# Modulation sums, chunked projections and a moved broadcast in a two-block transformer kernel

## What is computed

```python
def hybrid_layer(x, c, ...):
    mod = silu(c) @ mod_w + mod_b                       # 1024 x 6144
    shift1, scale1, gate1, shift2, scale2, gate2 = split(mod, 6)
    h = rms_norm(x, g_pre_mix) * (1 + scale1) + shift1
    sc_b, sc_c, sc_x, q, k, v, z, xbc, dt, gl_a, gl_b, gl_c = split_columns(h @ w_in)
    y_a = short_conv_mixer(sc_b, sc_c, sc_x, sc_conv_w) @ w_sc_out
    y_b = stick_breaking_attention(q, k, v) @ w_sb_out
    y_c = mamba2_mixer(z, xbc, dt, ...) @ w_ssm_out     # conv, silu, decay scan, gated norm
    merged = sigmoid(gl_a) * y_a + sigmoid(gl_b) * y_b + sigmoid(gl_c) * y_c
    x = x + gate1 * rms_norm(merged @ w_o, g_post_mix)
    h2 = rms_norm(x, g_pre_ffn) * (1 + scale2) + shift2
    gt, up = split(h2 @ w_ffn_in, 2)
    return x + gate2 * rms_norm((silu(gt) * up) @ w_ffn_out, g_post_ffn)

def second_block(x, c, ...):    # own modulation; attention, pooling, then peer_ffn:
    ...                         # top-16 of 16384 experts per head and token, gathered rows
```

## Time and profile before

| what | us |
|---|---|
| median of 3 runs | 1389.44 (1386.64 to 1390.31) |
| profiled execution | 1389.17 |
| its span | 1387.4 |
| PE busy | 1157.2 (83%) |
| DVE busy | 906.1 (65%) |
| POOL busy | 432.2 (31%) |
| ACT busy | 249.1 (18%) |
| DMA | 412.99 MB, mean 298 GB/s |

### The profile page before, as it was taken

One profiled execution on the slowest core, in us unless ns is written; L12 is line 12 of the kernel. 1 busy time (PEld: TensorE's weight loads), 2 busy tenths in 40 slices (PEclk: granted clock), 3 DMA queues, 4 the chain that ended last, 5 costly groups with the idle time before them and its releaser, 6 DMA issues.

```text
span 1387.4 us, 13536 instructions
## 1 busy us (share of the span) xinstructions
PE 1157.2 (83%) x4534; PEld 759.1 (55%) x4534; DVE 906.1 (65%) x2145; ACT 249.1 (18%) x412; POOL 432.2 (31%) x351
## 2 busy tenths in 40 slices
PE   2999898985799997798798998787878778777786
PEld 2888787845699996774374563333323333333332
DVE  7334037257788886543268869687786968778556
ACT  1114121015233333432211100101010010101001
POOL 0000000012244443220032536444444445445440
PEclk9999999998899998798898999898989998999998
DMA  9447335363667776230259999999999999999994
GB/s 387 179 144 275 155 141 199 148 236 128 261 278 291 293 299 242 71 112 31 91 227 421 418 396 421 421 421 421 421 422 420 421 420 422 422 421 422 421 422 166
DMA packets 57220, 412.99 MB, mean 298 GB/s; under 512 B 6480, under 2 KB 6480, under 8 KB 7120
## 3 DMA queue, kind: packets, MB, share of 16 engines
q0 software_dynamic: 42912, 311.97, 54.7%
q1 hardware_dynamic: 14256, 100.37, 18.7%
HBM read 411.26 MB, written 1.05 MB: 297 GB/s over the span
## 4 chain that ended last, share of the span: by engine, by line
PE 49%; DMA 27%; DVE 16%; issue 4%; ACT 2%; POOL 1%; DVEq 0%; SPq 0%; POOLq 0%; ACTq 0%
PE ps L394 13%; PE ps L815 11%; DMA areaB<-in_experts,idx 6%; DMA gate_area<-in_experts,idx 5%; PE ps L407 5%; PE ps L409 5%; PE ps L408 5%; DMA hT<-in_experts,idx 4%; PE ps L474 4%; DVE mod_sum L1214 3%; DMA ring<-in_experts,idx 3%; DMA mod_ring<-in_experts,idx 3%; DMA mod_ring<-in_mod_w 2%; PE ps L622 2%; DMA spare<-in_experts,idx 2%
## 5 line engine op out<-in xcount | busy, mean ns | idle before, releaser
L394 PE MATMUL ps<-hT,ring 128*128 128x256 f32 x960 | 220.2, 391 | 1.5 <-ACT hT L863 1.5
L394 PEld LDWEIGHTS ps<-hT,ring 128*128 128x128 f32 x960 | 187.8, 197 | 30.6 <-issue 3.9
L815 PE MATMUL ps<-areaB,mod_sum 128*128 128x512 f32 x304 | 157.4, 667 | 39.0 <-DVE mod_sum L1655 39.0
L815 PE MATMUL ps<-gate_area,mod_sum 128*128 128x512 f32 x240 | 118.8, 644 | 32.1 <-DVE mod_sum L1655 32.1
L815 PEld LDWEIGHTS ps<-areaB,mod_sum 128*128 128x128 f32 x304 | 63.1, 213 | 127.0 <-issue 76.5
L1156 POOL DMA_INDIRECT areaB<-in_experts,idx x76 | 92.3, 1215 | 112.6 <-PE ps L815 105.8
L1058 ACT ACTIVATE act<-now 128x2 f32<-128x2 f32 (+1 forms) x130 | 26.4, 203 | 562.4 <-DVE now L1646 562.4
L407 PE MATMUL ps<-hT_h,w_lo 128*128 128x256 f32 x416 | 119.0, 286 | 4.1 <-DVE hT_l L1199 2.2
L815 PE MATMUL ps<-ring,mod_sum 128*128 128x512 f32 x188 | 95.2, 653 | 31.9 <-DVE mod_sum L1655 31.9
L1646 DVE CUSTOM_DVE_ANT_0 areaB<-areaB,xn 128x1024 f32<-128x1024 f32 x76 | 92.2, 1223 | 44.4 <-DMA areaB<-in_experts,idx 44.3
L1214 DVE SCALAR_TENSOR_TENSOR mod_sum<-mod_ring,cols,mod_sum 128x256 f32<-128x256 f32 x294 | 119.2, 481 | 0.0
(11 more groups left out here) (273 smaller groups left out, 1855.1 us busy)
## 6 DMA issues: line engine op xcount, KB each, us to landing
ring<-in_stream SPq DMA_DIRECT2D x84, 1024.0 KB, 5.7
mod_ring<-in_mod_w POOLq DMA_DIRECT2D x40, 1024.0 KB, 6.9
gate_area<-in_mod_w SPq DMA_DIRECT2D x3, 1024.0 KB, 12.8
areaB<-in_mod_w SPq DMA_DIRECT2D x3, 1024.0 KB, 19.2
mod_ring<-in_mod_w SPq DMA_DIRECT2D x2, 1024.0 KB, 6.0
small<-in_small SPq DMA_DIRECT2D x1, 1352.0 KB, 27.4
areaB<-in_experts,idx POOLq DMA_INDIRECT x76, 22.6
x_sb<-in_x SPq DMA_DIRECT2D x1, 1024.0 KB, 9.0
```

The lines of the kernel that those rows point to most:

```text
L394: last = mm(ps[:, bank, b * T:(b + 1) * T], w[:, at:at + P], rhs[:, k, :], start=(k == 0), stop=(k == KC - 1))
L815: last = mm(ps[:, B3 + 2 * t + b, :], spread_w[n // FEW % 2][:, n % FEW, :], row[ROW_OF[n]][:, D + 512 * b:D + 512 * b + 512], start=first ...
```

## The change

- `mod_sum` gets eight places, so a pair from 8 on waits only for `mod_used` m - 6 (at least 8). `MOD_FRONT` = 28: pairs 24 and 26 come before the FFN, and POOL loads units 8 to 29 in one loop ahead of all its `split_lo` steps.
- DVE's pairs stand at: 8 after `dt_lin`; 10 after `ya`; 12 and 14 after sb_lk; 16 and 18 after sba (L1368); 20 after the acs copy, ahead of the wait for `acs_mm`; 22 after the weighting; 24 ahead of the merges; 26 after them. PE sums 8 to 11 after gl 3, 12 to 15 after the acs_mm matmuls, 16 to 19 after gl 11, 20 to 27 after wo 3.
- Head: the first eight units are stored so that each pair holds the same 256 columns of shift1 and scale1. After each pair `early_columns` makes two chunks' columns (inside the next pair's products), ACT makes all eight hT chunks, and PE does xbc 0 to 2 in parts (`xbc_part`) as chunks arrive, in three banks. The dt matmuls come after sc 0. SP's order is now: pair 0, x, small constants, pairs 1 and 2, slots 0 and 1, pair 3, slot 2, late constants.
- The first gate-row broadcast is done in halves after wo 0 and wo 1.

```diff
+MOD_FRONT = 28
-        mod_sum = sb("mod_sum", 4 * T)
+        mod_sum = sb("mod_sum", 8 * T)
+        def early_bank(j):
+            return (BM, BX, BM, BM)[j]
         def sum_place(m):
-            return m % 4 if m < 24 else m % 2
+            if m < MOD_EARLY:
+                return m % 4
+            return m % 8 if m < MOD_FRONT else m % 2
...
+            load_pair(0)
+            sp.dma_start(x_sb, x).then_inc(x_in, 16)
+            sp.dma_start(sm[:, n_c:n_late], small[:, n_c:n_late]).then_inc(small_in, 16)
+            load_pair(1)
+            load_pair(2)
+            first_load(0)
+            first_load(1)
+            load_pair(3)
+            first_load(2)
...
             transposes(0)
-            mod_units(*range(2, 8))
+            mod_units(2, 3)
+            def xbc_part(j, *ks):
+                w = arrived("xbc", j)
+                for b in range(2):
+                    for k in ks:
+                        pe.wait_ge(hT_act, k + 1)
+                        at = (b * KC + k) * P
+                        last = mm(ps[:, (0, 1, BX)[j], b * T:(b + 1) * T], w[:, at:at + P], hT[:, k, :],
+                                  start=(k == 0 and b == 0), stop=(k == KC - 1), skip_group_check=True)
+                if KC - 1 in ks:
+                    last.then_inc(unit_done, 1)
+            xbc_part(0, 0, 1)
+            xbc_part(0, 2, 3)
+            mod_units(4, 5)
+            xbc_part(0, 4, 5)
+            xbc_part(1, 0, 1, 2, 3, 4, 5)
+            pe.wait_ge(mod_read, 2)
+            xbc_part(2, 0, 1)
+            mod_units(6, 7)
+            xbc_part(2, 2, 3, 4, 5)
             for j in range(3):
-                proj_T("xbc", j)
+                xbc_part(j, 6, 7)
+            proj_T("sc", 0)
+            pe.wait_ge(evac, 3)
...
                     last.then_inc(acs_mm, 1)
-                    mod_units(14, 15)
+                    mod_units(*range(12, 16))
...
-            pe.wait_ge(yms, 1)
-            broadcast_row(0)
+            mod_units(*range(16, 20))
...
                 wide("wo", j, mT)
-                if j in (0, 2):
-                    mod_units(20 + j, 21 + j)
+                if j < 2:
+                    broadcast_half(0, j)
+            mod_units(*range(20, MOD_FRONT))
...
                     elif m >= 4:
-                        dve.wait_ge(mod_used, m - 2 if m < 24 else m)
+                        dve.wait_ge(mod_used, m - 2 if m < MOD_EARLY else max(MOD_EARLY, m - 6))
...
+            def early_columns(j):
+                dve.wait_ge(small_in, 16)
+                dve.wait_ge(mod_used, 2 * j + 2)
...
+            for m in range(1, MOD_EARLY // 2):
+                mod_units(2 * m, 2 * m + 2, lambda: early_columns(m - 1))
+            early_columns(MOD_EARLY // 2 - 1)
...
-            mod_units(12, 14)
+            mod_units(12, 16)
             dve.wait_ge(sb_sum, 1)
...
+            mod_units(16, 20)
             dve.wait_ge(acs_col_mm, 1)
             V.tensor_copy(dtb[:, 176:192], ps[:, BX, 0:16]).then_inc(acs_read, 1)
-            mod_units(14, 16)
+            mod_units(20, 22)
             dve.wait_ge(acs_mm, 1)
...
             split_lo(SPLIT0 + 2)
             hidden(0)
-            mod_units(24, 26)
             hidden(1)
             split_lo(SPLIT0 + 3)
             split_lo(SPLIT0 + 4)
-            mod_units(26, 28)
```

More of the change, by code:

```diff
@@ L320, in _, with load_pair, first_load @@
             sp.dma_start(sm[:, 0:n_c], small[:, 0:n_c]).then_inc(c_in, 16)
[L321 to L327, removed]
-                sp.dma_start(slot[s], stream[s]).then_inc(w_in[s], 16)
+            def load_pair(j):
+                for m in (2 * j, 2 * j + 1):
+                    sp.dma_start(mod_place(m), mod_w[m]).then_inc(mod_arrived(m)[0], 16)
+            def first_load(s):
+                sp.dma_start(slot[s], stream[s]).then_inc(w_in[s], 16)
+            load_pair(0)
[7 more added lines that the diff above has]
+            first_load(2)
             sp.dma_start(sm[:, n_late:], small[:, n_late:]).then_inc(late_in, 16)
@@ L373, in mod_sum_over_partitions @@
                 for b in range(2):
-                    o = columns[b] if columns else ps[:, BM, 2 * m + b:2 * m + b + 1]
+                    if m < MOD_EARLY and not columns:
+                        at = 8 * (m % 2) + 2 * (m // 2) + b
+                        o = ps[:, early_bank(m // 2), at:at + 1]
+                    else:
+                        o = columns[b] if columns else ps[:, BM, 2 * m + b:2 * m + b + 1]
                     at = T * sum_place(m) + b * P
@@ L491, in _ @@
             last.then_inc(dt_mm, 1)
-            for j in range(3):
+            for j in range(1, 3):
                 proj_T("sc", j)
@@ L519, in _ @@
                 proj_T("z", j)
-            mod_units(10, 11)
             for j in range(12):
@@ L523, in _ @@
                 if j == 3:
-                    mod_units(12, 13)
+                    mod_units(*range(8, 12))
                 if j == 2:
@@ L1237, in mod_units @@
                     vec = cols[:, 48 + 8 * (m // 24):56 + 8 * (m // 24)]
-                    for ins in mod_products([mod_place(m), mod_place(m + 1)], sum_place(m), vec, step.wait):
+                    for at, ins in enumerate(mod_products([mod_place(m), mod_place(m + 1)], sum_place(m), vec,
+                                                          step.wait)):
                         step(ins)
+                        if at == 7 and between:
+                            between()
+            def early_columns(j):
+                dve.wait_ge(small_in, 16)
+                dve.wait_ge(mod_used, 2 * j + 2)
+                here, bias, summed = (v.rearrange("p (g c) -> p g c", g=2)[:, :, 2 * j:2 * j + 2]
+                                      for v in (modT[:, 0:16], c_("mod_b", 0, 16), ps[:, early_bank(j), 0:16]))
+                V.tensor_tensor(here, summed, bias, ALU.add).then_inc(mod_read, 1)
+                dve.wait_ge(mod_read, j + 1)
+                V.scalar_tensor_tensor(out=cols[:, 2 * j:2 * j + 2], in0=modT[:, 8 + 2 * j:10 + 2 * j], scalar=1.0,
+                                       in1=c_("g_pre_mix", 2 * j, 2 * j + 2), op0=ALU.add, op1=ALU.mult)\
+                    .then_inc(col_ready, 1)
+                V.tensor_copy(cols[:, 8 + 2 * j:10 + 2 * j], modT[:, 2 * j:2 * j + 2]).then_inc(col_ready, 1)
             def modulation(m0, m1):
```

85 lines of the change are left out of this document (38 added, 47 removed).

## The result

| what | us |
|---|---|
| before, median | 1389.59 (1386.64 to 1390.31, 4 runs) |
| after, median | 1367.12 (1365.17 to 1370.17, 4 runs) |
| ratio, 95% interval | 0.9844 (0.9820 to 0.9868) |
| profiled execution before, its span | 1389.17, 1387.4 |
| profiled execution after, its span | 1365.17, 1363.4 |

The change is faster by 1.6%; predicted were 1367.8, with a range of 1361 to 1377. The two profiled executions differ by 24.0, the medians by 22.5.

A forecast was written before the change was run, and what follows sets the result against it. The last 587 us, DMA-bound gathers, move as a block; in projections and scan PE is the bound. Terms -2.0 -0.95 -3.3 -0.7 -14.4 = -21.4 take the profiled 1389.17 to 1367.8, range 1361 to 1377.

The forecast's parts named there:

- The head: Kernel start through the xbc projections to sc 0: xbc 2 ends at 57.0, sc 0 starts at 58.5; -2.0.
- Until T: Up to the end of the acs matmuls (T): PE sums four units instead of six, -0.95, T at 194.2.
- The wait that takes the place: Scan's decay to wo 0: pair 20 delays the decay arguments, PE waits 3.6, old waits go; net -3.3.
- Both margins called narrow: In the scan behind T: DVE's ysq stays hidden from PE by 1.2, the first merge by 2.4.
- Output projection: Start of wo to the norm's squares: 30.3 becomes 29.6, -0.7.
- FFN: First FFN pairs, without pairs 24 and 26: down 1 done at 372.2 instead of 386.60, -14.4.
- The low clock that stays in the FFN: Rival in the FFN: its waits go but the low clock stays, 1374; chance 0.11.
- the full PE that draws less clock: Rival in the FFN: without gaps the chip grants less clock; 1408 at mean 0.80; chance 0.03.
- A head that wins nothing: Rival at the head: parts run 1.7 longer at low clock and sc 0 waits 3; 1371; chance 0.09.
- a scan that pays twice: Rival in the scan: late pair 22 loads or ysq bring a further wait of 2; 1372; chance 0.10.
- Smoother than counted: Rival: the head wins 4 and no slow stretch follows the new scan wait; 1363; chance 0.07.
- a lost load period: Rival in the scan: pair 16 or 18 slips, pair 20's load up to 17.9 late; 1385; chance 0.03.

The follow-up runs named there:

- Experiment 2: The kernel after, with pairs 24 and 26, their loads and sums back inside the first two FFN pairs; median 1379.83, ratio 0.9939.
- experiment 3: The kernel after, with only pair 26 back in the FFN and units 28 and 29 loaded behind it; median 1370.87, ratio 0.9870.
- 4: The kernel after, with slots 0 and 1 loaded behind pair 3 and PE finishing xbc 0 and 1 before xbc 2; median 1361.08, ratio 0.9793.
- experiment 6: The kernel after, with the edits of experiment 1 and 4 together; median 1357.89, ratio 0.9772.
- experiment 1: The kernel after, with DVE's pair 20 moved behind the decay arguments and pair 22 behind ysq; median 1360.67, ratio 0.9790.
- experiment 7: Two single runs: kernel after with only slots 0 and 1 loaded behind pair 3, 1364.19; kernel before with only dt matmuls moved behind sc 0, 1391.34.

## Why the prediction was right

**The head.** The end of xbc 2 came at the predicted 57.0, sc 0 at 58.42 for 58.5, pair 3 at 32.86 for 32.8. The steps were right: order of loads, slot freed late. The first matmul came 1 earlier than said, which has no weight. The second profile of the same kernel (60.27) shows that the bounds of this term mattered more than its tenths.

**Until T.** The fewer sums gave 0.8 for 0.95 (z starts 3.7 ahead of before, gl 4 behind the sums 4.5); the predicted 194.2 was nevertheless 1.5 late. The missing step is the dt matmuls. The prediction said of them that they "only change places", and took over the time behind them, which in before held a slow stretch of 1.7 (12.2 against 10.5). After, it was not there. A duration taken from before carried a clock with it. That it would vanish could not be told from the trace: in other executions of the same head it is there, with 3.3 (experiments 2 and 3), and with 1.7 in 4 and 6.

**The wait that takes the place.** 3.6 was forecast, 3.54 came, by the queue that was named: pair 20 ahead of the arguments on DVE. The slow stretch behind it was mis-sized: 1.7 was taken from the rows behind the two old waits, 2.9 was measured (experiment 1 against after), though the kernels of 2 and 3 show 1.7 behind the same wait. From T to wo 0 it was nevertheless 81.5 for 81.2, since the rest of that chain had been counted 0.9 too long (gl 7, for one, ended at T+8.7, not T+9.0): the two errors nearly cancel. Both margins called narrow, ysq with 1.2 and the first merge with 2.4, held: PE shows no wait for them. The prediction's list of what goes (10.0) and what comes (6.25) makes -3.75, not the -3.3 of its sum; -3.0 was measured. It rightly priced the new wait but took it as given. That the wait could be avoided, by moving two pairs in DVE's program, is what experiment 1 adds.

The rule on waits between bursts (the Trainium skill, TensorE: Matmul & The Clock Gate, HAM oscillation) agrees with the slow rows behind the wait of 3.54. Here it goes only half the way: the same wait of 3.43 before wo 0 was followed by 7.13 in before, in after and in experiment 6, by a wo 0 of 8.83 in experiment 1 and of 10.20 in experiment 7, and the slow stretch behind the dt matmuls came without any wait.

**Output projection.** Squares came 29.5 behind the start of wo 0, predicted 29.6. **FFN.** 23.3 for 23.4. Experiment 2 shows that this part of the change makes it and that the wait for pair 26's load is in it; that the chain of loads, rather than the second pair as such, is most of it rests on the working at experiment 3. **Rivals.** The low clock that stays in the FFN (1374) falls, as does the full PE that draws less clock: the settled pair is 17.9, at a granted clock of 1.00. A head that wins nothing falls by 57.0 at xbc 2 and by sc 0, 2.1 ahead of where the dt matmuls began before; a scan that pays twice, by the missing second wait. "Smoother than counted" falls by the slow stretch of 2.9 behind the new wait, and a lost load period by DVE, which after the acs copy waited 14.15 for PE's sums and not for a load.

**The sum.** -21.4 predicted; -24.0 between the profiled executions, -22.5 between the medians. Of the 2.6 between forecast and profiled executions, 1.3 had come by down 1: 1.5 from the stretch behind the dt matmuls, less 0.2 in the later steps. Between down 1 and the end of the span another 1.3 came, which no step of the ledger covers and which is less than the spread of either kernel's runs. It came in the second block's attention: the squares behind the FFN start at 546.97 before and 524.85 after, 22.1 apart, and ACT's row at 699.46 before has its match at 675.17, 24.3 apart. The medians happen to lie closer to the forecast than the ledger does.

## What to carry to other kernels

Work that fills an engine's idle time is not free wherever the engine is idle, since others may wait for the instructions behind it: of two places that are both idle, take the one after the critical instructions. Here a pair put ahead of them cost 6.5, and behind them PE waited for nothing new. Look for chains in which a load waits for the product before it: one pair left in the FFN cost 2.2, two with a load between them 15.1. An early start on parts of the data is worth what it does to the end of the stage and to the release of its buffers. Finishing one buffer before opening the next, with the loads in the order of use, brought sc 0 forward by 3.6; the loads alone brought nothing.

## What the runs showed of the hardware

**Slow stretches.** The granted clock falls to 0.50, 1.2 GHz, for some 3 to 7 us (an estimate: twice the losses given here, of 1.7 to 3.3), and what one place costs differs from one execution to the next: behind the wait of 3.54, 2.9 or 1.7; behind the wait of 3.43 before wo 0, nothing, 1.7 or 3.1; behind the wait of 3.62 ahead of gl 5, 1.7 or nothing; behind the dt matmuls nothing, 1.7 or 3.3. The last ones follow no wait: in before, PE shows 2.00 of 2 busy in every slice from 60 to 72. A ledger of a single profiled execution is therefore good to some 3 us, whatever the tenths of its terms; the runs themselves spread over 5.0 (1365.17 to 1370.17 for after).

**Loads at the start.** In two executions of the same kernel the wait for sc 0's weights ended at 58.42 and at 60.27, with the same program ahead of it; the products of pair 3, behind their load, started at 32.86 and 33.40.
